# A hybrid decoder step: the ConvFFN as seven-multiplication block products in two stages, with the gated tiles kept in DRAM

## The chip, the cores and the metric

The kernel runs on one core of a Trainium2 chip. The metric is the device time of one execution in microseconds (us), median of three runs. TensorE (PE) multiplies, VectorE (DVE), ScalarE (ACT) and GpSimd (POOL) work elementwise, and SyncE (SP) issues the DMAs. SBUF is the on-chip memory; TensorE writes to PSUM, which has eight banks.

## What is computed

A prompt of 1024 tokens and eight samples of eight tokens (1088 columns together, held as features x tokens) go through two layers. Layer 0 has an attention and recurrence mixer, layer 1 a token-mixing MLP; each is followed by a gated ConvFFN with D_MODEL = 1024 and D_FF = 3072. causal_dwconv takes three taps over time and a bias; m_p and m_s are the mixer's outputs, DEPTH is 2:

```python
def conv_ffn(xn, buf, w_g, w_u, w_c, b_c, w_d):
    g = xn @ w_g
    gc, new_buf = causal_dwconv(g, buf, w_c, b_c)
    return (jax.nn.gelu(gc) * (xn @ w_u)) @ w_d, new_buf
...
    for l in range(DEPTH):
        ...
        yp = yp + m_p
        ys = ys + m_s
        fw = (w_gate[l], w_up[l], w_ffn_conv[l], b_ffn_conv[l], w_down[l])
        f_p, fb_p = conv_ffn(rmsnorm(yp, g_ffn[l]), fbuf_p, *fw)
        f_s, fb_s = conv_ffn(rmsnorm(ys, g_ffn[l]), state_ffn_conv[l], *fw)
        yp = yp + f_p
        ys = ys + f_s
```

Everything is fp32. A product is made to nearly fp32 precision with three passes over operands rounded to the fp32r type: each operand is split in a high part (its rounding, made on ACT) and a remainder (value minus high part), and the product is hi\*hi + lo\*hi + hi\*lo.

## The kernel before, in words

**Layout.** A tile is 128 features x tokens. The residual stream x lies in SBUF as eight such tiles (`core.x`, shown as x_residual, padded to 1092 columns). A weight slab is 128 x 1024. The slab loads run on SP, the high parts of slabs on ACT (L97, L104), their remainders on POOL (L108, L113).

**Gate and up.** `Ffn` works in twelve turns of two hidden tiles each. A turn has four dense products (`gu` in `Ffn.tensor`, by `dense`, L148): gate and up for two tiles, each 8 slabs deep x 3 passes x 3 column chunks (364, 364, 360) = 72 matmuls. DVE takes the gate sum from PSUM times the RMS scale in one instruction (`gate`, L2193), runs the convolution with 3 instructions over all columns and six small ones (`conv`, L2203 to L2220), ACT takes the GELU (L2112), POOL multiplies by the RMS scale that belongs to the up half (`gate_scale`, L1923), and DVE multiplies with the up sum from PSUM (L2227).

**Down.** The two hidden tiles of a turn, 256 deep, go at once into the down product, as a seven-multiplication (Strassen-Winograd) block product on 2 x 2 blocks: `tiles` makes the four block sums of the hidden tiles and seven remainders on DVE, `block` makes the four sums and the remainders of the weight blocks on POOL (L1940 to L1952). `quarter` (L1999 to L2011) runs 21 matmuls of 512 columns and four of 256 for the sample columns, four times in a turn; DVE adds each product from PSUM to x_residual (L2243). The twelfth turn's down product is dense (L2025). The quarters of turn t-1 stand between the dense products of turn t.

**Order.** Each engine has one hand-written queue; semaphores join them. On DVE a turn reads: gate, seven adds, convolution, gate, seven adds, convolution, up, seven adds, up, seven adds, tiles.

## Time and profile before

| | |
|---|---|
| median of 3 runs | 2642.78 us (2642.22 to 2642.88) |
| the profiled execution | span 2640.3 us |
| PE busy | 2589.7 us, 98% |
| DVE busy | 1606.4 us, 61% |
| POOL busy | 1133.4 us, 43% |
| ACT busy | 867.6 us, 33% |
| first ConvFFN, 638 to 1466 us | 828 us, of which PE busy 828 us |
| second ConvFFN | begins near 1792 us and runs almost to the end |

Matmuls are pipelined, so a busy PE says only that it never waited; the pace of a kind of matmul is the distance from start to start in the timeline. A mean duration on DVE or POOL contains what the instruction waited for once it had begun.

### The profile page before, as it was taken

The numbers are of one execution on the slowest core, as the hardware profiler recorded it, in microseconds if no ns is written. First come the engines' busy times: TensorE is split into PE (matmuls) and PEld (weight loads), VectorE is DVE, ScalarE is ACT, GpSimd is POOL, SyncE is SP. The second block draws the span as 40 slices with busy tenths as digits, with TensorE's granted clock in tenths as the row PEclk, the third lists the DMA queues.
The fourth block names the chain that finished last, engine by engine and source line by source line (L and its number), as shares of the span: only waits on it lengthen the run. The fifth ranks groups of instructions, "written<-read, shape, count | busy, mean of one in ns | idle before, by whom it ended". The sixth has DMA issues, their size and how long they took to land.

```text
span 2640.3 us, 42777 instructions
## 1 busy us (share of the span) xinstructions
PE 2589.7 (98%) x16013; PEld 2419.6 (92%) x16013; DVE 1606.4 (61%) x2183; ACT 867.6 (33%) x1229; POOL 1133.4 (43%) x919
## 2 busy tenths in 40 slices
PE   8999998899999999999999999999999999999999
PEld 7878886699999999999999999999999999999998
DVE  6456566533666666666676544524666677766674
ACT  5575666532222222222222524423222222222221
POOL 3233333224544454444555411344555555544541
PEclk9999999999999999999999999999999999999999
DMA  5101107731111111111111211211111111111112
GB/s 178 55 28 44 43 25 261 270 114 46 59 41 48 48 48 48 48 42 46 48 48 33 62 36 39 62 40 59 54 41 47 48 48 48 48 42 45 48 32 72
DMA packets 208445, 164.11 MB, mean 62 GB/s; under 512 B 9901, under 2 KB 182038, under 8 KB 208334
## 3 DMA queue, kind: packets, MB, share of 16 engines
q1 hardware_dynamic: 207278, 160.35, 19.5%
q10 hardware_dynamic: 576, 2.10, 0.2%
q8 instruction: 79, 1.29, 0.2%
q14 instruction: 32, 0.26, 0.0%
q0 software_dynamic: 480, 0.11, 0.0%
HBM read 147.83 MB, written 14.69 MB: 62 GB/s over the span
## 4 chain that ended last, share of the span: by engine, by line
PE 78%; DVE 0%; ACT 0%; issue 0%; DVEq 0%
PE psum_all L148 50%; PE psum_all L2011 16%; PE psum_all L2485 6%; PE psum_all L2025 2%; PE psum_all L1999 1%; PE psum_all L2001 1%; PE psum_all L2537 0%; PE psum_all L2501 0%; PE psum_all L2525 0%; PE psum_all L2355 0%; PE psum_all L2571 0%; PE psum_all L1679 0%; DVE mixed_odd L2696 0%; ACT operand_hi_a L1784 0%; PE psum_all L2542 0%
## 5 line engine op out<-in xcount | busy, mean ns | idle before, releaser
L108 POOL TENSOR_TENSOR w_lo_part<-w_raw,w_hi_part 128x1024 fp32r<-128x1024 f32 x94 | 227.4, 2419 | 578.1 <-ACT w_hi_part L104 578.1
L2243 DVE TENSOR_TENSOR x_residual<-x_residual,psum_all 128x512 f32<-128x512 f32 (+1 forms) x616 | 449.7, 760 | 19.6
L148 PE MATMUL psum_all<-operand_hi_c,w_hi_part 128*128 128x364 f32 (+1 forms) x1344 | 297.5, 330 | 0.6 <-DVE operand_lo_c L1788 0.6
L148 PE MATMUL psum_all<-operand_hi_a,w_hi_part 128*128 128x364 f32 (+1 forms) x1344 | 297.7, 330 | 0.2 <-DVE operand_lo_a L1788 0.2
L148 PE MATMUL psum_all<-operand_hi_c,w_lo_part 128*128 128x364 f32 (+1 forms) x1344 | 295.5, 328 | 0.0
L148 PE MATMUL psum_all<-operand_lo_a,w_hi_part 128*128 128x364 f32 (+1 forms) x1344 | 295.3, 328 | 0.0
L148 PE MATMUL psum_all<-operand_hi_a,w_lo_part 128*128 128x364 f32 (+1 forms) x1344 | 295.2, 328 | 0.0
L148 PE MATMUL psum_all<-operand_lo_c,w_hi_part 128*128 128x364 f32 (+1 forms) x1344 | 294.9, 327 | 0.0
L113 POOL TENSOR_TENSOR w_lo_part<-w_raw,w_hi_part 128x1024 fp32r<-128x1024 f32 x54 | 130.6, 2419 | 372.3 <-ACT w_hi_part L97 372.2
L2227 DVE TENSOR_TENSOR gate_conv_ffn<-psum_all,gate_conv_ffn 128x1092 f32<-128x1092 f32 x48 | 62.2, 1295 | 347.7 <-PE psum_all L148 347.7
L2011 PE MATMUL psum_all<-hidden_hi_ffn,w_down_hi_ffn 128*128 128x512 f32 x616 | 240.7, 391 | 0.0
L2011 PE MATMUL psum_all<-hidden_hi_ffn,w_down_lo_ffn 128*128 128x512 f32 x616 | 240.5, 390 | 0.0
L2011 PE MATMUL psum_all<-hidden_lo_ffn,w_down_hi_ffn 128*128 128x512 f32 x616 | 239.7, 389 | 0.0
L148 PEld LDWEIGHTS psum_all<-operand_hi_a,w_hi_part 128*128 128x128 f32 x1344 | 233.4, 188 | 4.2 <-DVE operand_lo_a L1788 0.5
L148 PEld LDWEIGHTS psum_all<-operand_hi_c,w_hi_part 128*128 128x128 f32 x1344 | 233.1, 188 | 4.4 <-issue 0.8
L148 PEld LDWEIGHTS psum_all<-operand_hi_c,w_lo_part 128*128 128x128 f32 x1344 | 233.4, 188 | 0.0
L148 PEld LDWEIGHTS psum_all<-operand_hi_a,w_lo_part 128*128 128x128 f32 x1344 | 233.2, 188 | 0.0
L148 PEld LDWEIGHTS psum_all<-operand_lo_a,w_hi_part 128*128 128x128 f32 x1344 | 232.2, 188 | 0.0
L148 PEld LDWEIGHTS psum_all<-operand_lo_c,w_hi_part 128*128 128x128 f32 x1344 | 232.2, 188 | 0.0
L104 ACT ACTIVATE w_hi_part<-w_raw 128x1024 fp32r<-128x1024 f32 x94 | 99.7, 1062 | 402.1 <-PE psum_all L148 402.1
L1923 POOL TENSOR_TENSOR gate_conv_ffn<-gate_conv_ffn,rms_scale 128x1092 f32<-128x1092 f32 x48 | 122.3, 2548 | 187.2 <-ACT gate_conv_ffn L2112 187.2
L1361 POOL TENSOR_TENSOR take_then_weights<-take_then_weights,x_residual 128x511 f32<-128x511 f32 (+3 forms) x96 | 96.0, 1010 | 158.4 <-DVE x_residual L1393 119.5
(354 smaller groups left out, 5031.6 us busy)
## 6 DMA issues: line engine op xcount, KB each, us to landing
w_raw<-in_w_gate_dram SPq DMA_DIRECT2D x48, 512.0 KB, 3.8
w_raw<-in_w_up_dram SPq DMA_DIRECT2D x48, 512.0 KB, 3.8
w_down_raw_ffn<-in_w_down_dram SPq DMA_DIRECT2D x44, 512.0 KB, 4.0
pages<-in_cache_k_dram SPq DMA_DIRECT2D x64, 256.0 KB, 3.5
pages<-in_cache_v_dram SPq DMA_DIRECT2D x64, 256.0 KB, 5.4
w_raw<-in_w_in_even_dram SPq DMA_DIRECT2D x20, 512.0 KB, 4.0
w_raw<-in_w_in_odd_dram SPq DMA_DIRECT2D x16, 512.0 KB, 4.8
x_spill<-x_residual SPq DMA_DIRECT2D x8, 546.0 KB, 5.3
```

The lines of the kernel that those rows point to most:

```text
L104: act.activation(dst, self.raw[:, raw, :], ACT.Copy).then_inc(self.s_hi, 1)
L108: pool.tensor_tensor(lo, self.raw[:, raw, :], hi.bitcast(F32), ALU.subtract).then_inc(self.s_lo, 1)
L113: pool.tensor_tensor(dst if dst is not None else self.lo[:, par, :], self.raw[:, par, :], (hi if hi is not None else self.hi[:, par, :]).b ...
L148: mm = pe.matmul(bank[:, c, 0:width(c)], w, x[:, chunk(c)], start=(k == 0 and step == 0), stop=(k == last and step == 2))
L1361: pool.tensor_tensor(t[:, 0:n - 1], t[:, 0:n - 1], k[:, 1:n], ALU.mult).then_inc(weighted, 1)
L1923: pool.tensor_tensor(gc, gc, self.core.rb[:, :], ALU.mult).then_inc(self.gr_ready, 1)
L1999: pe.matmul(rows, b.h_smp[:, k, :], self.blocks(b.d_hi, p, 0)[:, cols], start=start and p % 2 == 0 and k == 0, stop=False, skip_group_chec ...
L2011: mm = pe.matmul(core.ps[:, base + bank, :], wt, xt[:, x, :], start=first and step == 0, stop=step == 2, skip_group_check=True)
L2025: mm = pe.matmul(bank[:, c, 0:width(c)], wt, x[:, chunk(c)], start=(k == 0 and step == 0), stop=(k == 1 and step == 2))
L2227: dve.tensor_tensor(gc, bank[:, :, 0:CH], gc, ALU.mult).then_inc(self.evac, 1)
L2243: dve.tensor_tensor(dst, dst, src, op).then_inc(self.pair_read, 1)
L2485: mm = pe.matmul(self.core.ps[:, self.lane_bank(f), 0:width(c)], wm[:, is_u, col], xm[:, k, chunk(c)], start=k == 0 and s == 0, stop=k == ...
```

## The change

`Ffn` is replaced. A layer's ConvFFN now has two stages.

**Stage 1**, 24 jobs in 12 pairs (gate, then up, for two hidden tiles). A job multiplies a 1024 x 256 slab by all 1088 columns as a seven-multiplication product on 2 x 2 blocks: the weights in blocks of 128 columns, x in blocks of odd or even tiles by 544 columns. Its seven products have 4 x 3 x 2 = 24 matmuls of 272 columns. Weight side, per job: four block sums and seven remainders of 512 columns on POOL (`block_sums`, `block_lo`), seven high parts on ACT (`block_hi`). x side: seven operands made once in a layer, while the output projection before it ends (`tile_lo`, `open_dve`, `opening_dve`). The results go from PSUM to SBUF: four parts copied by ACT (`copy_out`), three added by DVE (`add_out`). The RMS scale of the gate is now an instruction of its own on DVE (`conv_part`, L2413), and the hidden tile is the product of two SBUF tiles (`hidden_tile`). Four block sums of the hidden tiles are made on DVE (`hidden_sum`), and the seven block operands are stored in DRAM (`store_hidden`). The space for all this is that of x: x is spilled to DRAM at the start of the layer's ConvFFN and loaded again before stage 2.

**Stage 2**, 16 jobs in 4 rounds of 4. A round takes three hidden pairs (768 deep), loads their seven operands from DRAM, splits them (high parts on ACT, remainders on DVE, `piece_hi`, `piece_lo`), and a job multiplies them by 256 columns of w_down: seven products of 3 x 3 x 2 = 18 matmuls of 272 columns, added to x by DVE (`add_residual`). Weight sums and remainders are 384 columns on POOL.

PE's waits between the seven products of a stage 1 job n stand in `tensor`: product 1 waits until the three DVE adds of job n-1 are done (`dve_out` 3n), product 3 for DVE's add of product 1. A layer has 6048 matmuls of 272 columns in place of 3456 of 364 or 360, 924 of 512, 176 of 256 and 144 dense ones. The dense projections of the mixers stay; their other passes end at column 1088 and no longer at 1092.

```diff
+    def block_sums(self, pool, n, first, second):
+        if first:
+            pool.wait_ge(self.w_in[n % 2], 16 * (n // 2 + 1))
+            if n:
+                pool.wait_ge(self.w_lo, 7 * n)
+            pool.tensor_tensor(self.sums(n, "S1"), self.part(n, 0, 1), self.part(n, 1, 1), ALU.add
+                               ).then_inc(self.w_sum, 1)
...
+    def block_lo(self, pool, n, i):
+        pool.wait_ge(self.w_hi, self.done(n, i))
...
+    def gate_scale(self, pool, t, r):
+        pool.wait_ge(self.gelu_ready, 2 * t + r + 1)
+        pool.tensor_tensor(self.conv[:, r, :], self.conv[:, r, :], self.core.rb[:, 0:USED], ALU.mult
+                           ).then_inc(self.gr_ready, 1)
...
+        for n in range(JOBS):
+            t = n // 2
+            up, last = n < JOBS1 and n % 2, n == JOBS - 1
+            for i in range(7):
+                if not last:
+                    if i < 3:
+                        self.block_sums(pool, n + 1, i == 0, (None, "S2", "S4")[i])
+                    self.block_lo(pool, n + 1, i)
+                if up and i in (3, 5):
+                    self.gate_scale(pool, t, (i - 3) // 2)
...
+        dve.wait_ge(self.dve_out, 6 * t + 2 + r)
+        g = gb[:, 2:2 + USED]
+        o.did(dve.tensor_tensor(g, g, self.core.rb[:, 0:USED], ALU.mult))
+        o.did(dve.tensor_copy(xs[:, :, 0:2], self.params.state[:, f, :].rearrange("p (s j) -> p s j", j=2)))
+        o.after()
+        if t:
+            dve.wait_ge(self.hc, 16 * t)
+        o.did(dve.tensor_scalar(gc, g, tap(2), tap(3), ALU.mult, ALU.add))
...
+        for t in range(PAIRS):
+            last = t == PAIRS - 1
+            if t:
+                for i in (1, 4, 6):
+                    self.add_out(dve, 2 * t, i)
+            self.conv_part(dve, o, t, 0)
+            self.add_out(dve, 2 * t + 1, 1)
+            self.conv_rest(dve, o, t, 0)
+            self.conv_part(dve, o, t, 1)
+            self.conv_rest(dve, o, t, 1)
+            self.add_out(dve, 2 * t + 1, 4)
+            if last:
+                self.piece_lo(dve, 0, B21)
+                self.piece_lo(dve, 0, B11)
+            self.hidden_tile(dve, t, 0)
+            self.hidden_sum(dve, t, T1)
+            self.add_out(dve, 2 * t + 1, 6)
+            if not last:
+                self.hidden_tile(dve, t, 1)
+                for i in (T3, T2, NT4):
+                    self.hidden_sum(dve, t, i)
...
+                if n < JOBS1:
+                    if i == 0:
+                        pe.wait_ge(self.act_out, 4 * n)
+                    elif i == 1:
+                        pe.wait_ge(self.dve_out, dve)
+                    elif i == 3:
+                        pe.wait_ge(self.dve_out, dve + 1)
```

On DVE, before, a gate tile's work at the start of a turn (gate_padded_ffn is the gate tile, gate_conv_ffn the convolved one):

```order
L2193 TENSOR_TENSOR gate_padded_ffn<-psum_all,rms_scale 128x1092
L2203 TENSOR_SCALAR gate_conv_ffn<-gate_padded_ffn,ffn_params 128x1092
L2204 COPY gate_sample_ffn<-ffn_state_columns 128x8x2
L2206 COPY gate_sample_ffn<-gate_padded_ffn 128x8x8
L2210 SCALAR_TENSOR_TENSOR gate_conv_ffn<-gate_padded_ffn,ffn_params,gate_conv_ffn 128x1092 x2
L2213 TENSOR_SCALAR gate_conv_ffn<-gate_sample_ffn,ffn_params 128x64
L2214 COPY new_state_columns_ffn<-gate_padded_ffn 128x2
L2215 COPY new_state_columns_ffn<-gate_sample_ffn 128x16
```

On DVE now, the end of an up job and the beginning of the next pair (gate, up and convolved tiles all lie in x_residual's space):

```order
L2401 TENSOR_TENSOR x_residual<-x_residual,psum_all 128x544
L2445 TENSOR_TENSOR x_residual<-x_residual 128x1088
L2454 TENSOR_TENSOR x_residual<-x_residual 128x544
L2401 TENSOR_TENSOR x_residual<-x_residual,psum_all 128x1088
L2445 TENSOR_TENSOR x_residual<-x_residual 128x1088
L2454 TENSOR_TENSOR x_residual<-x_residual 128x544 x3
L2401 TENSOR_TENSOR x_residual<-x_residual,psum_all 128x544 x2
L2401 TENSOR_TENSOR x_residual<-x_residual,psum_all 128x1088
L2413 TENSOR_TENSOR x_residual<-x_residual,rms_scale 128x1088
L2414 COPY gate_sample<-ffn_state_columns 128x8x2
L2418 TENSOR_SCALAR x_residual<-x_residual,ffn_params 128x1088
```

The scale by rms_scale has lost its PSUM input; both its inputs are in SBUF now. The fourth row is the last add of the up job; it stands behind the first hidden tile (second row) and its sum.

On POOL, before, the end of the first turn's weight work:

```order
L1923 TENSOR_TENSOR gate_conv_ffn<-gate_conv_ffn,rms_scale 128x1092
L108 TENSOR_TENSOR w_lo_part<-w_raw,w_hi_part 128x1024
L1923 TENSOR_TENSOR gate_conv_ffn<-gate_conv_ffn,rms_scale 128x1092
L108 TENSOR_TENSOR w_lo_part<-w_raw,w_hi_part 128x1024
L1940 TENSOR_TENSOR square_scratch<-w_down_raw_ffn 128x128
L1941 TENSOR_TENSOR square_scratch<-w_down_raw_ffn 128x128
```

On POOL now, what stands beside one up job (the weights of the gate job after it, and the two scalings of the gated tiles):

```order
L2058 TENSOR_TENSOR block_sums_a<-w_raw 128x512
L2060 TENSOR_TENSOR block_sums_a<-w_raw 128x512
L2075 TENSOR_TENSOR blocks<-w_raw,blocks 128x512
L2064 TENSOR_TENSOR block_sums_b<-block_sums_a,w_raw 128x512
L2075 TENSOR_TENSOR blocks<-w_raw,blocks 128x512
L2068 TENSOR_TENSOR block_sums_b<-w_raw,block_sums_b 128x512
L2075 TENSOR_TENSOR blocks<-block_sums_a,blocks 128x512
L2075 TENSOR_TENSOR blocks<-block_sums_b,blocks 128x512
L2081 TENSOR_TENSOR x_residual<-x_residual,rms_scale 128x1088
L2075 TENSOR_TENSOR blocks<-block_sums_b,blocks 128x512
L2075 TENSOR_TENSOR block_a_7980<-w_raw,block_a_7980 128x512
L2081 TENSOR_TENSOR x_residual<-x_residual,rms_scale 128x1088
```

A scaling stands in POOL's queue ahead of remainders that do not depend on it.

## Rows read from the trace of the kernel before

**Rows 1.** The page, part 1: busy time, share of the span and instructions of each engine.
```profile
PE 2589.7 (98%) x16013; PEld 2419.6 (92%) x16013; DVE 1606.4 (61%) x2183; ACT 867.6 (33%) x1229; POOL 1133.4 (43%) x919
```
**Rows 2.** Busy time by stretch, the first ConvFFN: PE, PEld, DVE, ACT, POOL, clock, DMA.
```profile
638.00:1466.00 828.00, 828.00 (x4692) 789.87 (x4691) 554.02 (x744) 198.67 (x273) 413.46 (x343) 1.00 0.15 47
```
**Rows 3.** PE's own waits behind 560 us (total, times, longest): the longest one.
```profile
PE psum_all L2355 <- DVE y_rows L2381: 1.6, 2, 0.9
```
**Rows 4.** Timeline of PE (start, duration, then what): matmuls of 364, 256 and 512.
```profile
801.19 0.66 PE L148 MATMUL psum_all<-operand_hi_a,w_lo_part 128*128 128x364 f32 x3
...
803.67 0.28 PE L1999 MATMUL psum_all<-w_down_hi_ffn,hidden_sample_ffn 128*128 128x256 f32 x1
...
804.14 0.40 PE L2011 MATMUL psum_all<-hidden_hi_ffn,w_down_hi_ffn 128*128 128x512 f32 x1
...
805.97 0.39 PE L2011 MATMUL psum_all<-hidden_lo_ffn,w_down_hi_ffn 128*128 128x512 f32 x1
```
**Rows 5.** Timeline of DVE and of POOL around 862 us.
```profile
861.99 1.36 DVE L2203 TENSOR_SCALAR gate_conv_ffn<-gate_padded_ffn,ffn_params 128x1092 f32<-128x1092 f32 x1
863.27 1.26 DVE L2204 COPY gate_sample_ffn<-ffn_state_columns 128x16 f32 x1
...
861.47 1.29 POOL L1949 TENSOR_TENSOR w_down_lo_ffn<-w_down_raw_ffn,w_down_hi_ffn 128x512 fp32r<-128x512 f32 x1
862.72 1.77 POOL L1952 TENSOR_TENSOR w_down_lo_ffn<-square_scratch,w_down_hi_ffn 128x512 fp32r<-128x512 f32 x1
```
**Rows 6.** Timeline of DVE and of POOL around 1437 us.
```profile
1437.16 1.66 DVE L2284 TENSOR_TENSOR hidden_lo_ffn<-gate_conv_ffn,hidden_hi_ffn 128x1092 fp32r<-128x1092 f32 x1 [1.74 <-ACT hidden_hi_ffn L2137]
...
1435.26 5.84 POOL L108 TENSOR_TENSOR w_down_lo_ffn<-w_raw,w_down_hi_ffn 128x1024 fp32r<-128x1024 f32 x2 [8.43 <-ACT w_down_hi_ffn L104]
```
**Rows 7.** Timeline of DVE and of POOL around 995 us.
```profile
994.43 5.35 DVE L2243 TENSOR_TENSOR x_residual<-x_residual,psum_all 128x512 f32<-128x512 f32 x7
...
994.86 2.41 POOL L108 TENSOR_TENSOR w_lo_part<-w_raw,w_hi_part 128x1024 fp32r<-128x1024 f32 x1
997.22 0.47 POOL L1940 TENSOR_TENSOR square_scratch<-w_down_raw_ffn 128x128 f32<-128x128 f32 x1
997.64 0.47 POOL L1941 TENSOR_TENSOR square_scratch<-w_down_raw_ffn 128x128 f32<-128x128 f32 x1
```
**Rows 8.** Groups by shape on DVE behind 560 us (count, busy, mean ns, idle before).
```profile
L2243 DVE TENSOR_TENSOR x_residual<-x_residual,psum_all 128x512 f32<-128x512 f32 x528 | 342.4, 683 | 12.6
L2210 DVE SCALAR_TENSOR_TENSOR gate_conv_ffn<-gate_padded_ffn,ffn_params,gate_conv_ffn 128x1092 f32<-128x1092 f32 x96 | 130.5, 1359 | 12.3 <-DVE gate_sample_ffn L2206 6.1
L2243 DVE TENSOR_TENSOR x_residual<-x_residual,psum_all 128x1024 f32<-128x1024 f32 x88 | 107.5, 1221 | 6.9
L2213 DVE TENSOR_SCALAR gate_conv_ffn<-gate_sample_ffn,ffn_params 128x64 f32<-128x64 f32 x48 | 15.6, 324 | 1.8
```
**Rows 9.** One line's instructions on DVE or POOL: duration ns min/median/max.
```profile
L2218 DVE SCALAR_TENSOR_TENSOR gate_conv_ffn<-gate_sample_ffn,ffn_params,gate_conv_ffn x24: 283/286/1270, 661.9 to 1422.5; 128x64 f32<-128x64 f32 x24
...
L1923 POOL TENSOR_TENSOR gate_conv_ffn<-gate_conv_ffn,rms_scale x24: 2532/2552/2576, 663.7 to 1424.3; 128x1092 f32<-128x1092 f32 x24
...
L1949 POOL TENSOR_TENSOR w_down_lo_ffn<-w_down_raw_ffn,w_down_hi_ffn x44: 1282/1292/1322, 682.0 to 1412.4; 128x512 fp32r<-128x512 f32 x44
```
**Rows 10.** Groups by shape on ACT behind 560 us, as rows 8.
```profile
L2119 ACT ACTIVATE w_down_hi_ffn<-w_down_raw_ffn 128x512 fp32r<-128x512 f32 x88 | 54.9, 624 | 176.1 <-PE psum_all L2011 176.1
L2112 ACT ACTIVATE gate_conv_ffn<-gate_conv_ffn 128x1092 f32<-128x1092 f32 x48 | 53.6, 1117 | 232.9 <-DVE gate_conv_ffn L2220 232.9
```
**Rows 11.** Timeline of PE, and stretches as rows 2: an idle TensorE and its clock.
```profile
472.70 2.22 PE L1017 MATMUL psum_all<-identity,pages 128*128 128x128 f32 x12 [1.52 <-DVE x_residual L1526]
...
474.00:476.00 2.00, 2.00 (x12) 2.00 (x11) 0.78 (x2) 0.78 (x2) 0.00 (x0) 0.50 0.83 203
477.00:480.00 3.00, 3.00 (x28) 0.98 (x20) 0.00 (x0) 0.39 (x2) 0.00 (x0) 1.00 0.77 259
466.00:468.00 2.00, 1.61 (x12) 0.85 (x8) 1.97 (x2) 1.44 (x4) 0.00 (x0) 1.00 1.06 405
```

More of the change, by code:

```diff
@@ L1792, in scalar @@
         w, n0 = self.core.w, self.n0
-        for m in range(KT):
-            w.split_hi(act, n0 + m + 2, (n0 + m + 2) // 2, m % 2, (w.used, n0 + m + 3 - self.skew))
-            self.lead.tile_act(act, m)
+        for m in range(KT - 2):
+            w.split_hi(act, n0 + m + 2, (n0 + m + 2) // 2, m % 2, self.job_done(m))
+            self.ffn.tile_act(act, m)
             if m == 0:
@@ new lines, in multiply @@
+    def multiply(self, pe, n, i, ready=None):
+        name, first = self.GROUPS[i]
+        b = self.banks[name]
+        depth = self.depth(n)
+        x_hi, x_lo = self.operand(n, i, 0), self.operand(n, i, 1)
+        w_hi, w_lo = self.block(n, i, 0), self.block(n, i, 1)
+        order = [(q, s) for s in range(3) for q in range(depth)]
+        if ready:
+            order = [(q, s) for q in range(depth) for s in range(3)]
+        mm = None
+        for at, (q, s) in enumerate(order):
+            if ready and s == 0:
+                ready(q)
+            wt, xt = ((w_hi, x_hi), (w_lo, x_hi), (w_hi, x_lo))[s]
+            for h in range(2):
+                mm = pe.matmul(self.core.ps[:, b + h, 0:HB], wt[:, q * P:(q + 1) * P], xt[:, q, HB * h:HB * (h + 1)],
+                               start=first and at == 0, stop=at == len(order) - 1, skip_group_check=True)
+        mm.then_inc(self.product, 1)
@@ new lines, in tile_dve, with tile_lo @@
+    def tile_dve(self, dve, m, held=None):
+        for which, (i, h) in enumerate(((B21, 0), (B22, 1)) if m % 2 else ((B11, 0),)):
+            if not (m == held and which):
+                self.tile_lo(dve, m, which, i, h)
+    def tile_lo(self, dve, m, which, i, h):
+        q = m // 2
+        dve.wait_ge(self.b_hi, 3 * q + 1 + (m % 2) + which)
+        dve.scalar_tensor_tensor(self.operand(0, i, 1)[:, q], self.half(self.core.x[:, m, :], h), self.gain(m),
+                                 self.operand(0, i, 0)[:, q].bitcast(F32), ALU.mult, ALU.subtract).then_inc(self.b_lo, 1)
@@ new lines, in add_out @@
+    def add_out(self, dve, n, i):
+        dve.wait_ge(self.product, self.done(n, i))
+        dve.wait_ge(self.act_out, 4 * n + {1: 1, 4: 3, 6: 4}[i])
+        if i == 6:
+            dst = self.target(n, 1).rearrange("p (c h n) -> p c h n", c=2, h=2)
+            src = self.group("a").unsqueeze(1).to_broadcast((P, 2, 2, HB))
+        else:
+            dst = self.half(self.target(n, 0), i == 4).rearrange("p (h n) -> p h n", h=2)
+            src = self.group("a" if i == 1 else "bb")
+        dve.tensor_tensor(dst, dst, src, ALU.add).then_inc(self.dve_out, 1)
@@ new lines, in add_residual @@
+    def add_residual(self, dve, n, i):
+        m = n - JOBS1
+        base, p = 3 * JOBS1 + 7 * m, m % QUARTERS
+        top, low = self.core.x[:, 2 * p, :], self.core.x[:, 2 * p + 1, :]
+        if m < QUARTERS and i == 0:
+            dve.wait_ge(self.x_back[p], 32)
+        dve.wait_ge(self.product, self.done(n, i))
+        if i in (1, 4, 6):
+            dve.wait_ge(self.dve_out, base + {1: 1, 4: 4, 6: 6}[i])
+        if i == 6:
+            dst = low[:, 0:USED].rearrange("p (c h n) -> p c h n", c=2, h=2)
+            src = self.group("a").unsqueeze(1).to_broadcast((P, 2, 2, HB))
+        else:
+            tile, h = ((top, 0), (top, 0), (low, 1), (top, 1), (top, 1), (low, 0))[i]
+            dst = self.half(tile, h).rearrange("p (h n) -> p h n", h=2)
+            src = self.group(self.GROUPS[i][0])
+        dve.tensor_tensor(dst, dst, src, ALU.add).then_inc(self.dve_out, 1)
@@ L2827, in _ @@
             params1.load(sp)
-            out1.slabs(sp)
+            out1.sync(sp)
             ffn1.sync(sp)
```

1325 lines of the change are left out of this document (718 added, 607 removed).

## The prediction

> **What bounds the kernel now.** Read the busy shares first: PE is busy for 98% of the span, DVE for 61%, POOL for 43% [rows 1]. Then the stretch of the first ConvFFN: 828 us, and PE busy in all of them [rows 2]. Then PE's own waits: behind 560 us the longest kind comes to 1.6 us in total [rows 3]. So the ConvFFNs are bound by PE's stream, and since a busy PE is no pace, the pace comes from distances of starts [rows 4]: 15 matmuls of 364 or 360 columns in 803.67 - 801.19 = 2.48 us, 165 ns each; 4 of 256 in 0.47 us, 118 ns; 8 of 512 in 1.83 us, 229 ns. From 364 to 512 that is 0.43 ns a column and a fixed part of some 10 to 15 ns.
>
> **PE's new stream.** No row has 272 columns. From the 256 row, 118 + 16 x 0.43 = 125 ns; down from the 364 row, 165 - 91 x 0.42 = 127 ns. I take 127 (it is the longer, and the 256 row is only four matmuls); 125 to 129 is the range. A stage 1 product has 24 matmuls, 3.05 us; a job 7 of them, 21.35 us; a pair 42.7 us. A stage 2 job is 126 x 0.127 = 16.0 us. A layer: 6048 x 0.127 = 768 us against 828 [rows 2], 60 us less, 120 us for both. The seven-for-eight saving on gate and up is partly paid back by the narrower matmul.
> The Trainium skill (TensorE: Matmul & The Clock Gate, section "Wait — 56ns, not 53.3ns?") puts the fixed part of a warm matmul at about 2.5 ns. By that a 272-column one would be an estimated 116 ns and a layer 700 us. The rows above show 10 to 15 ns for these fp32r matmuls with a weight load each, so the page's figure isn't used.
>
> **What DVE and POOL do to each other.** This decides the case. At 861.99 a DVE tensor_scalar over 1092 columns begins while POOL's remainder (861.47 + 1.29) runs; POOL's next one, begun at 862.72, takes 1.77 us in place of a median of 1.29 [rows 5, 9]. The 16-column copy behind it takes 1.26 us and ends with that POOL instruction. At 1437.16 a DVE tensor_tensor with both inputs in SBUF takes 1.66 us, and two POOL remainders together 5.84 us where one alone takes 2.41 [rows 6, 7]: 1.02 us too long. A small DVE instruction of 0.28 us takes up to 1.27 [rows 9]. But seven DVE adds with one input in PSUM take 5.35 us beside a POOL instruction that still takes 2.41 [rows 7]. I read: POOL's tensor_tensors exclude DVE instructions with two SBUF inputs, and copies and plain tensor_scalars in SBUF; whoever came first finishes, then the other. PSUM adds are free of it.
> The change moves work under this lock. Pure durations: POOL 1.26 us start to start for 512 columns [rows 5], hold 1.15; 2.55 us for a gate scaling [rows 9], hold 2.4. A pair has 22 of the first (8 sums, 14 remainders; that a sum of four pieces of 128 costs no more than a remainder is assumed) and 2 of the second: 30 us held. DVE: 683 and 1221 ns for 512 and 1024 columns [rows 8] are 1.05 ns a column and 0.15 fixed, so 544 columns take 0.7 us and 1088 1.3, held for 0.6 and 1.15; a tap with a second tensor is alike (1359 ns for 1092, [rows 8]); the first tap, a tensor_scalar, runs at double pace, since at 862.72 it had still to run and was done at 863.35: 0.6 us [rows 5]. Per tile: RMS scale 1.15, three taps 0.6 + 1.15 + 1.15, small ones 0.2; per pair two tiles, two hidden tiles 2.3 and four sums 2.3: 13 us held. Together 43 us of the 42.7 that PE gives; before, a turn of two hidden tiles had 828 / 12 = 69 us.
>
> **One pair walked through.** Zero is the end of the gate job's last product. ACT takes 0.63 us for a high part and for a 544-column copy, 1.1 for a GELU [rows 10]. In DVE's queue stand: last add of the gate job, first tile's scale and two taps, add of the up job's product 1, rest of the first convolution, the whole second one, add 4, hidden tile, hidden sum, last add.
> - Last add 0 to 1.3. POOL's remainder of the last block 0.7 to 1.9. Scale 1.9 to 3.1, POOL sum to 4.2, copy, POOL sum to 5.4, first tap to 6.0, POOL remainder to 7.1, copy, POOL sum to 8.3, second tap to 9.5, add to 10.2. Product 3 could begin at 9.15 and waits 1.1 us.
> - POOL remainder to 10.5, third tap to 11.75, POOL sum to 12.8, two copies and POOL's remainder to 14.1, small ones to 14.8. GELU to 15.9; POOL's remainder meanwhile to 15.8, the second tile's scale to 17.0, gate scaling (POOL) to 19.3, copy, remainder to 20.5, first tap to 21.1, remainder to 22.3; then POOL waits for the second GELU, and DVE alone finishes at 26.5.
> - Add 4 to 27.2, hidden tile to 28.4, POOL's second gate scaling to 30.8, hidden sum to 31.4, last add to 32.7. PE ended the up job at 10.25 + 4 x 3.05 = 22.45 and product 0 of the next at 25.5; its product 1 needs that last add: 7.2 us of waiting.
> - Hidden tile and three sums, each behind one POOL instruction, to 40.0; the add of product 1 to 40.7, and product 3, ready at 38.85, waits 1.9 us. Four products more: the pair ends at 52.95.
> So a pair takes 53.0 us, 10.2 of them waits of PE, 245 us in 24 pairs. Without the lock the same DVE queue takes about 18 us and all three waits vanish. ACT has some 15 us of work in a pair and SP's stores stay behind loads needed a job later; 47 MB more a layer are some 50 GB/s in 900 us, where the trace has 405 [rows 11]: no term.
> PE's idle time has a second price: behind 1.52 us of waiting in a thin stretch its granted clock is 0.50, that is 1.2 of 2.4 GHz, from 474 to 476, and 1.00 from 477 [rows 11]. Here some 3 us at half clock behind the 7 us wait cost 1.7 us in products 1 and 2, which the 1.9 us wait absorbs: I take nothing; if it doesn't, 0 to 2 us a pair.
>
> **The rest of a layer.** Opening: T2's remainder needs x tile 7, seven DVE instructions and 2176 columns after it, some 13 us, where PE has three products, 9.1 us; with T3's end 7 us (0 to 15). Step to stage 2: add 4, two remainders of 1632 columns (683 x 1632 / 512 is 2.2 us at most, 1.8 by the slope), hidden tile and sum stand ahead of the last add, and each product waits for its own remainder; some 22 us of waits, 9 of which are already in the twelfth pair: 13 us (5 to 25). Three changes of round: seven remainders, 12.6 us, and 5.2 us of adds plus turns with POOL in a 16 us job: 4 us each, 12 (0 to 25). Work on the next mixer's operands in the last round: 3 us. Other stage 2 jobs wait for nothing: their adds read PSUM.
>
> **The sum.** 12 x 53.0 = 636; 16 x 16.0 = 256; 7 + 13 + 12 + 3 = 35: 927 us a layer against 828, 99 more, 198 for both. The profiled execution's span, 2640.3 us, becomes 2838; the median lies 2.5 above that span: 2841, given as **2840**. Its own range, with pairs of 50 to 56 us and the bounds above: 2760 to 2920.
>
> **The rivals.**
> *The lock doesn't reach PE* (faster): POOL has slack inside a job, its blocks are needed a job later, and if DVE mostly goes first, its chain from the gate job's end to the last add stays under 24.4 us (21.35 + 3.05), the point from which PE waits. Then pairs take 42.7 to 43.5: 768 to 780 plus 25 = 800 a layer, 2585; 2550 if the steps cost little. For it: DVE's own work there is 18 us. Against it: the copy at 863.27 lost its turn to a POOL instruction that already waited [rows 5], and POOL waits nearly always here.
> *Half of it*: the chain takes 28 us in place of 33 (fewer encounters, or POOL idle for longer than I have). Pairs of 47.5: 570 + 256 + 35 = 861, two layers 66 more: 2710.
> *It is worse*: the clock falls at each wait and isn't absorbed, and four-piece sums cost 1.7 us as the four single ones before did (a 128-column one starts 0.42 us after another, [rows 7]); pairs of 57: 684 + 256 + 60 = 1000, 2985.
>
> **How the numbers follow.** Forecast 0.60, no effect of the lock 0.17, half 0.15, worse 0.08. Range for 8 in 10: 2600 to 2910, which leaves out the first rival's most and the worst case. A measurement of this kernel can tell about 0.2% from no change, 5 us. Faster: the first rival and a fifth of the half case, 0.20; the same 0.02; slower 0.78.
>
> **What would show it.** In the profile after: PE's waits led by a DVE add on x_residual, some 7 us and 24 times, and one of 1 to 2 us twice a pair; pairs 53 us apart; DVE copies of 16 columns and taps with means far over their minima; POOL over 70% busy; PE's clock under 1.00 in many stretches. A start-to-start of 272-column matmuls of 125 to 129 ns shows the first step; 116 would refute it. If DVE's waits on POOL don't show in those means, the forecast is wrong from its base; if they do and PE still waits under 2 us a pair, the walk is.

## The result and the profile after

The changed kernel takes 2859.69 us (median of four runs, 2859.14 to 2864.93) against 2642.59 for the kernel before on the same chip: 1.0829 times as long, 95% interval 1.0814 to 1.0844. The forecast was 2840 and its range 2600 to 2910. The profiled execution has a span of 2857.4 us.

The page's part 1, and the row of TensorE's clock in its 40 slices, answer to [rows 1]:
```profile
PE 2534.9 (89%) x18693; PEld 2421.1 (85%) x18693; DVE 1870.5 (65%) x1846; ACT 1081.0 (38%) x1611; POOL 1764.4 (62%) x1175
...
PEclk9999999998899899899999999998998998999999
```
PE issues more matmuls than before and is busy 55 us less, so the span, 217 us longer, lies in PE's idle time. PE's own waits over the whole run (total, times, longest), which answer to [rows 3]:
```profile
PE psum_all L2136 <- DVE x_residual L2401: 206.2, 55, 11.1
PE psum_all L2136 <- DVE x_residual L1827: 14.5, 2, 7.2
PE psum_all L2136 <- DVE ffn_x L2370: 14.4, 2, 7.5
PE psum_all L2136 <- DVE down_x_ffn L2086: 9.1, 2, 4.8
```
L2401 is the add from PSUM in `add_out`. One pair in PE's timeline (start, duration, then what; in brackets the idle time ahead and what ended it), as [rows 4] are read:
```profile
884.38 8.03 PE L2136 MATMUL psum_all<-ffn_x,blocks 128*128 128x272 f32 x48 [7.27 <-DVE x_residual L2401]
892.76 6.24 PE L2136 MATMUL psum_all<-ffn_x,blocks 128*128 128x272 f32 x48 [0.35 <-DVE x_residual L2401]
898.84 3.16 PE L2136 MATMUL psum_all<-ffn_x,block_a 128*128 128x272 f32 x24
901.84 3.16 PE L2136 MATMUL psum_all<-ffn_x,block_s 128*128 128x272 f32 x24
904.84 9.16 PE L2136 MATMUL psum_all<-ffn_x,blocks 128*128 128x272 f32 x72
915.54 6.24 PE L2136 MATMUL psum_all<-ffn_x,blocks 128*128 128x272 f32 x48 [1.53 <-DVE x_residual L2401]
921.62 3.16 PE L2136 MATMUL psum_all<-ffn_x,block_a 128*128 128x272 f32 x24
924.62 3.16 PE L2136 MATMUL psum_all<-ffn_x,block_s 128*128 128x272 f32 x24
927.62 3.16 PE L2136 MATMUL psum_all<-ffn_x,blocks 128*128 128x272 f32 x24
938.14 12.13 PE L2136 MATMUL psum_all<-ffn_x,blocks 128*128 128x272 f32 x76 [7.36 <-DVE x_residual L2401]
```
The pair is 938.14 - 884.38 = 53.76 us. Its three waits are ahead of product 1 of the gate job (7.27), product 3 of the gate job (0.35) and product 3 of the up job (1.53). Between 898.84 and 904.84 two products of 24 matmuls start 3.00 us apart, 125 ns a matmul.

DVE in the same pair, same columns, from the gate job's last add on:
```profile
905.04 1.29 DVE L2401 TENSOR_TENSOR x_residual<-x_residual,psum_all 128x1088 f32<-128x1088 f32 x1 [5.28 <-PE psum_all L2136]
...
914.68 0.71 DVE L2401 TENSOR_TENSOR x_residual<-x_residual,psum_all 128x544 f32<-128x544 f32 x1
...
922.41 2.51 DVE L2414 COPY gate_sample<-ffn_state_columns 128x16 f32<-128x16 f32 x1
...
936.71 1.27 DVE L2401 TENSOR_TENSOR x_residual<-x_residual,psum_all 128x1088 f32<-128x1088 f32 x1
```
The last add of the up job ends at 937.98; PE was ready for it at 930.8. A copy of 16 columns takes 2.51 us on the way. What it waited for, on DVE and on POOL:
```profile
920.11 2.38 DVE L2413 TENSOR_TENSOR x_residual<-x_residual,rms_scale 128x1088 f32<-128x1088 f32 x1
...
921.41 3.47 POOL L2081 TENSOR_TENSOR x_residual<-x_residual,rms_scale 128x1088 f32<-128x1088 f32 x1
```
This is one exchange of turns: DVE's scale runs until 922.49; POOL's scaling, begun at 921.41, ends at 924.88, 2.4 us after DVE's; and the copy behind DVE's scale, begun at 922.41, ends at 924.92, with POOL's instruction. Groups on DVE by shape from 700 to 1150 us (count, busy us, mean ns, idle before), as [rows 8]:
```profile
L2454 DVE TENSOR_TENSOR x_residual<-x_residual 128x544 f32<-128x544 f32 x33 | 67.0, 2029 | 1.1
L2413 DVE TENSOR_TENSOR x_residual<-x_residual,rms_scale 128x1088 f32<-128x1088 f32 x17 | 36.6, 2155 | 0.0
L2421 DVE SCALAR_TENSOR_TENSOR x_residual<-x_residual,ffn_params 128x1088 f32<-128x1088 f32 x17 | 32.5, 1914 | 0.6
...
L2414 DVE COPY gate_sample<-ffn_state_columns 128x16 f32<-128x16 f32 x17 | 29.1, 1713 | 0.0
...
L2419 DVE COPY gate_sample<-x_residual 128x64 f32<-128x64 f32 x17 | 24.2, 1426 | 0.0
L2401 DVE TENSOR_TENSOR x_residual<-x_residual,psum_all 128x544 f32<-128x544 f32 x33 | 23.5, 712 | 52.0 <-PE psum_all L2136 52.0
```
The hidden sum of 544 columns with both inputs in SBUF means 2029 ns, the add of 544 columns with one in PSUM 712.

Last, PE's clock behind the long wait, in stretches as [rows 11]:
```profile
884.40:888.40 4.00, 4.00 (x18) 4.00 (x19) 3.96 (x2) 0.00 (x0) 4.00 (x3) 0.51 0.21 84
888.40:892.40 4.00, 4.00 (x32) 3.79 (x31) 3.93 (x4) 0.64 (x1) 4.00 (x3) 1.00 0.14 56
```
After 7.27 us of idle time the granted clock is 0.51, 1.2 of 2.4 GHz, and 18 matmuls start in 4 us in place of 32.

### The profile page after: what moved, and what is told of

It is laid out like the page before. It is cut to its first block, busy times and chain, and to the rows that moved or that the text cites. A ratio compares the mean times of both kernels' runs of the same rounds, so it can differ in the third digit from the quotient of the medians.

```text
span 2857.4 us, 46273 instructions
## 1 busy us (share of the span) xinstructions
PE 2534.9 (89%) x18693; PEld 2421.1 (85%) x18693; DVE 1870.5 (65%) x1846; ACT 1081.0 (38%) x1611; POOL 1764.4 (62%) x1175
## 4 chain that ended last, share of the span: by engine, by line
PE 46%; DVE 23%; issue 8%; POOL 3%; ACT 1%; DVEq 0%; ACTq 0%; POOLq 0%
PE psum_all L2136 32%; PE psum_all L2697 6%; PE psum_all L148 6%; DVE x_residual L2401 3%; DVE x_residual L2431 3%; DVE x_residual L2413 2%; DVE x_residual L2418 2%; DVE gate_sample L2414 2%; DVE x_residual L2445 2%; DVE gate_sample L2419 2%; DVE x_residual L2421 1%; DVE x_residual L2454 1%; DVE x_residual L2434 1%; DVE new_state_columns L2435 1%; POOL blocks_down L2075 1%
## 5 line engine op out<-in xcount | busy, mean ns | idle before, releaser
L2136 PE MATMUL psum_all<-ffn_x,blocks 128*128 128x272 f32 x5760 | 802.3, 302 | 240.0 <-DVE x_residual L2401 203.0
L2136 PEld LDWEIGHTS psum_all<-ffn_x,blocks 128*128 128x128 f32 x5760 | 784.6, 202 | 253.3 <-POOL block_s L2075 169.8
L2136 PE MATMUL psum_all<-down_x_ffn,blocks_down 128*128 128x272 f32 x2880 | 380.2, 292 | 31.0 <-DVE down_x_ffn L2086 9.1
L2136 PEld LDWEIGHTS psum_all<-down_x_ffn,blocks_down 128*128 128x128 f32 x2880 | 371.0, 191 | 37.3 <-issue 28.7
L113 POOL TENSOR_TENSOR w_lo_part<-w_raw,w_hi_part 128x1024 fp32r<-128x1024 f32 x52 | 126.9, 2441 | 358.4 <-ACT w_hi_part L97 358.3
L2473 DVE TENSOR_TENSOR x_residual<-x_residual,psum_all 128x544 f32<-128x544 f32 (+1 forms) x224 | 178.6, 798 | 223.1 <-PE psum_all L2136 222.0
L2401 DVE TENSOR_TENSOR x_residual<-x_residual,psum_all 128x544 f32<-128x544 f32 x144 | 129.9, 902 | 281.8 <-PE psum_all L2136 265.2
L2081 POOL TENSOR_TENSOR x_residual<-x_residual,rms_scale 128x1088 f32<-128x1088 f32 x48 | 154.0, 3208 | 113.2 <-ACT x_residual L2261 112.1
L2454 DVE TENSOR_TENSOR x_residual<-x_residual 128x544 f32<-128x544 f32 x96 | 185.1, 1928 | 3.2
L2697 PE MATMUL psum_all<-operand_a,w_hi_part 128*128 128x364 f32 (+1 forms) x672 | 169.9, 331 | 0.0
L909 PE MATMUL psum_all<-in_hi_even,w_hi_part 128*128 128x384 f32 (+1 forms) x456 | 157.0, 344 | 1.2 <-DVE xb_padded L1430 0.6
```

Source lines behind the costliest of these rows:

```text
L113: pool.tensor_tensor(dst if dst is not None else self.lo[:, par, :], self.raw[:, par, :], (hi if hi is not None else self.hi[:, par, :]).b ...
L909: mm = pe.matmul(bank(key, 0, b - a), wt[:, n % 2, col], xt[:, k, a:b], start=k == 0 and s == 0, stop=k == KT - 1 and s == 2)
L2081: pool.tensor_tensor(self.conv[:, r, :], self.conv[:, r, :], self.core.rb[:, 0:USED], ALU.mult).then_inc(self.gr_ready, 1)
L2136: mm = pe.matmul(self.core.ps[:, b + h, 0:HB], wt[:, q * P:(q + 1) * P], xt[:, q, HB * h:HB * (h + 1)], start=first and at == 0, stop=at = ...
L2401: dve.tensor_tensor(dst, dst, src, ALU.add).then_inc(self.dve_out, 1)
L2454: dve.tensor_tensor(dst, x, y, op).then_inc(self.hid, 1)
```

## The experiments

Theory: DVE and POOL take turns at SBUF, so that each DVE instruction with two SBUF inputs, and each copy, waits for a POOL instruction; this makes the chain to the up job's last add longer than the 24 us that PE leaves it. Rivals: the add comes too late by its place in DVE's queue, whatever the lengths; or DVE's own work is too long. The edits are shown shortened, and "..." stands for lines left out.

**One cause taken away: the remainders don't read SBUF.**
```
-  pool.tensor_tensor(block(n, i, 1), source(n, i), block(n, i, 0), ALU.subtract)
+  for q in range(4):                       # stage 1 only
+      mm = pool.memset(block(n, i, 1)[:, q * P:(q + 1) * P], 0.0)
```


> The changed kernel with one edit: in stage 1 POOL's fourteen weight remainders a pair are four memsets of 128 columns each in place of one subtraction of 512, so the remainders of gate's and up's weights are zero (that part of the computation is left out); POOL still writes as many columns, but reads nothing from SBUF there. Theory (POOL's SBUF reads exclude DVE's two-input instructions and copies): POOL holds the lock for 8 sums and 2 scalings a pair, 14 us in place of 30; the 16-column copies on DVE fall from a mean of 1.66 us to under 0.9, the last add comes some 6 us earlier, PE's 7.3 us wait falls to 0 to 3, pairs take 43 to 47 us in place of 53.8, and the whole some 2600 to 2700 us. Rival (DVE's queue is too long by itself, in the order it is written): nothing changes, 2860. Rival (POOL's own lateness holds PE): PE's waits on DVE stay and those on POOL go, under 10 us in all.

Measured: 2703.34 us, 1.023 of before (1.021 to 1.0251). 156 us of the loss are gone, and the time lies just above the expected range. The pair is 47.7 us: the 7.3 us wait has become 1.73, and 1.99 and 1.24 us are left ahead of the two products 3. The profile puts the 1.99 down to POOL (in all such waits of the run 39.9 us, 20 times), but the POOL instruction that ended then, at 880.05, fills a block of the next job; DVE's add of the up job's product 1, which product 3 waits for, ended at 880.02, and PE went on at 880.16. So it is the changed kernel's 1.53 us wait ahead of that product, and the third outcome expected as possible, lateness of POOL itself, isn't shown. The sums and the gate scaling still read SBUF, and DVE's hidden sums still mean 2026 ns, while its 16-column copy fell from 1713 to 718.

**All of POOL's reads in stage 1 taken away.**
```
+  def fill(pool, dst, inc):                # block sums, remainders, gate scaling
+      four memsets of a quarter of dst's columns each
```


> The changed kernel with everything that GpSimd reads from SBUF in stage 1 taken away: the remainders, the block sums S1 to S4 and the gate scaling are each written as four memsets of a quarter of the columns. Left out of the computation are therefore stage 1's remainders, its block sums and the scaling of the gate; every wait, every weight-block conversion, all 48 DVE instructions of a pair and all TensorE work stand. Theory (DVE and GpSimd exclude each other instruction by instruction when both read SBUF, and that alone makes DVE late): DVE's instructions all fall to their own lengths (16 columns far under 1 us, sums L2459-like and taps to some 1.3 us), TensorE hardly waits inside a pair, a pair takes 42.7 to 44.5 us instead of 53.8 and 47.7 without the remainders alone; 24 pairs x (53.8 - 43.5) = 247, and some 12 from the two openings: 2600, range 2575 to 2640. Rival (what is left of the wait is the chain product, copy, add, three taps, product and comes from the order of DVE's work): the pair stays near 47.7 and the time near 2700.

Measured: 2564.37 us, 0.9707 of before (0.9686 to 0.9727), below the expected range. PE's row from 700 to 1150 us (PE, PEld, DVE, ACT, POOL, clock, DMA share, GB/s), and under it three groups of DVE as above:
```profile
700.00:1150.00 450.00, 450.00 (x3579) 450.00 (x3578) 243.01 (x352) 157.56 (x254) 183.63 (x995) 1.00 0.29 101
```
```profile
L2478 DVE TENSOR_TENSOR x_residual<-x_residual 128x544 f32<-128x544 f32 x40 | 29.0, 724 | 1.4
L2437 DVE TENSOR_TENSOR x_residual<-x_residual,rms_scale 128x1088 f32<-128x1088 f32 x21 | 27.0, 1285 | 0.0
...
L2438 DVE COPY gate_sample<-ffn_state_columns 128x16 f32<-128x16 f32 x21 | 5.2, 249 | 0.0
```
PE never stops; the pair is 42.3 us. DVE does 352 instructions in 243 us where the changed kernel did 290 in 349 (its row from 700 to 1150 is shown below). Its program is the same, and so is its order, so the order alone does no harm and DVE's own work fits. POOL still writes SBUF, by 988 memsets that hold it for 176 of the 450 us, and the two-input instructions never lengthen beside them: the 40 sums lie between 724 and 726 ns, the 21 scales between 1283 and 1286. It is POOL's reading that excludes these. The short copies do still wait for a memset: the 2-column copy takes 0.33 us beside one (at 730.14) and 0.16 beside none (at 723.82).

The edit changes one thing more: POOL's busy time falls from 346 to 184 us, so its results are ready earlier. But in the changed kernel DVE stood idle ahead of the hidden tiles, the ones that need POOL's result, for only 1.8 us of the 450, so this can't be the gain.

**The order of DVE's adds.** In the changed kernel add 4 and add 6 of the up job stand behind the whole second gate tile.
```
   self.conv_part(dve, o, t, 1)
+  self.add_out(dve, 2 * t + 1, 4)
+  self.add_out(dve, 2 * t + 1, 6)
   self.conv_rest(dve, o, t, 1)
-  self.add_out(dve, 2 * t + 1, 4)
   ...
   self.hidden_tile(dve, t, 0)
   self.hidden_sum(dve, t, T1)
-  self.add_out(dve, 2 * t + 1, 6)
```


> The changed kernel with DVE's adds 4 and 6 of the up job moved ahead, between the second tile's first two taps and the rest of its convolution. Nothing is left out. Theory (PE's 7.3 us wait is for the position of the last add in DVE's queue, behind instructions that the lock draws out): that wait falls to under 1.5 us. But the hidden tile and sums come later by as much, and the gate job's product 3 waits for the add behind them: from 0.4 us to 3 to 6. Pairs 49 to 51 us in place of 53.8, some 2740 to 2800 us. Rival (the wait just moves): 2860. Rival (the add's position is all there is): pairs of 44, 2640.

Measured: 2881.42 us, 1.0904 (1.0873 to 1.0934): 0.8% slower than the changed kernel. This expectation failed, and the rival that the wait just moves was right, but for the 22 us more. The wait went to the next add in the queue:
```profile
892.52 7.71 PE L2136 MATMUL psum_all<-ffn_x,blocks 128*128 128x272 f32 x48 [8.57 <-DVE x_residual L2401]
...
947.12 3.29 PE L2136 MATMUL psum_all<-ffn_x,blocks 128*128 128x272 f32 x13 [8.56 <-DVE x_residual L2401]
```
This is product 3 of the gate job, which waits for add 1 of the same job, now behind everything that was put off. So that add goes forward too:
```
   the edit above, and
-  for i in (1, 4, 6): self.add_out(dve, 2 * t, i)
+  for i in (4, 6): self.add_out(dve, 2 * t, i)
   ...
   self.hidden_sum(dve, t, T1)
+  self.add_out(dve, 2 * t + 2, 1)
   self.hidden_tile(dve, t, 1)
```


> As the run before, and the gate job's add of product 1 stands ahead of the second hidden tile and the last three sums. Nothing is left out. Theory: both waits go, what is left is product 3 of the up job, 1.5 us, and what a later POOL adds to the next pair, 0 to 3 us: pairs 44 to 47 us, 2625 to 2700 us. Rival (DVE and POOL together are saturated, the pair is bound by the lock's total of 43 us plus turns lost, whatever the order): pairs of 50 and more, over 2770.

Measured: 2729.42 us, 1.0329 (1.0312 to 1.0347), somewhat above the expected range. The pair is 47.7 us, with 2.4 and 1.3 to 1.5 us of waits. The 96 matmuls behind the 2.36 us wait take 917.93 - 904.44 = 13.49 us in place of 12.0, since the clock falls there too (904.40 to 906.40, as above):
```profile
904.40:906.40 2.00, 1.96 (x9) 1.99 (x10) 1.90 (x5) 0.00 (x0) 0.00 (x0) 0.50 0.65 221
```

**Copies that don't take turns.** The four small DVE copies of a gate tile, written as a sum over an axis of one element.
```
-  dve.tensor_copy(dst, src)
+  dve.tensor_reduce(dst, src.unsqueeze(-1), AxisListType.X, ALU.add)
```


> The changed kernel with the four small copies of each hidden tile on DVE (16, 64, 2 and 16 columns) written as tensor_reduce over an axis of one element, which gives the same values. Nothing is left out. Theory (a copy in SBUF waits for POOL's turn, a tensor_reduce doesn't): the three copies of means 1.66, 1.38 and 0.74 us fall to 0.2 to 0.3 each; part of it comes back as a longer wait of the next instruction, since POOL still takes turns; PE's 7.3 us wait falls to 1 to 5 us, pairs 48 to 52 us, 2720 to 2820 us. Rival (the reduce waits as the copy does): the means stay, 2860. Rival (all waits come back in the taps): means fall and the time stays.

Measured: 2823.7 us, 1.0686 (1.0664 to 1.0707), 36 us less than the changed kernel and just above the expected 2720 to 2820. Groups on DVE, 700 to 1150 us:
```profile
L2426 DVE SCALAR_TENSOR_TENSOR x_residual<-x_residual,ffn_params 128x1088 f32<-128x1088 f32 x17 | 46.4, 2732 | 0.6
...
L1639 DVE TENSOR_REDUCE gate_sample<-x_residual 128x64 f32<-128x64 f32 x17 | 3.5, 206 | 0.0
L1639 DVE TENSOR_REDUCE gate_sample<-ffn_state_columns 128x16 f32<-128x16 f32 x17 | 2.7, 157 | 0.0
```
The 16-column copy fell from 1713 ns to 157, the 64-column one from 1426 to 206. But the tap behind them, 1914 ns in the changed kernel (L2421 there), is now 2732: where a copy had waited for POOL, the next instruction that takes turns waits. The four copies of a tile became 3.4 us shorter; its other convolution instructions and the scale became 2.5 us longer together by their means. That leaves 0.9 a tile, 1.7 a pair, and the pair (52.1 us) became 1.6 shorter. The rival that the waits come back in the taps was right for the larger part.
The Trainium skill (SBUF — State Buffer, section "Who interferes with whom") says that tensor_reduce on trn2 never contends with GpSimd. The 157 and 206 ns agree.

**Edits together.** First the early adds and the copies by reduction.

> The two edits that gave something, together: the adds of product 4 and 6 of the up job and of product 1 of the next gate job earlier in DVE's queue (2729 alone), and the four small copies of a gate tile as sums over an axis of one element (2824 alone against 2860). Nothing is left out. Theory of the lock with turns: short copies that wait a GpSimd instruction each cost some 8 x 0.6 us of DVE a pair, but part of it comes back in the next two-input instructions; the wait that is left after the early adds is 3.8 us a pair, and the copies can give at most 1.5 (what they gave alone: 36 us in 24 pairs) : 2690 to 2725. Rival (the early adds left TensorE waiting on something that the copies don't stand in front of): 2725 to 2735, as without the copies.

Measured: 2662.83 us, 1.0081 (1.0064 to 1.0098), better than either theory had it. The two edits gave 130 and 36 us alone and 197 together.

The third edit moves the gate scaling to DVE, so that one multiplication by DVE takes the place of one by POOL:
```
-  if up and i in (3, 5): self.gate_scale(pool, t, (i - 3) // 2)
   def hidden_tile(self, dve, t, r):
+      self.gate_scale(dve, t, r)
```
With the early adds:

> The early adds, and the scaling of the gate tile by the token's factor on DVE just ahead of the product with u, instead of on GpSimd (L2081, two of 3.24 us in a pair). Nothing is left out. Theory (what counts is the time that both engines together hold the way to SBUF): a GpSimd multiplication of 1088 columns of some 2.4 us on its own goes, a DVE one of some 1.3 us comes, so the sum held falls by 2.2 us a pair, up to 24 x 2.2 = 53 us of the 84 us of waits that are left: 2680 to 2725. Rival (what counts is the length of DVE's own queue, 41.5 us of 54 busy): 2 x 1.3 us or more are added to it ahead of the adds, and the time rises by 24 x 1 to 2.6: 2750 to 2790.

Measured: 2669.08 us, 1.0102 (1.0085 to 1.0119), below the range of the first theory, which was the nearer by far. From 700 to 1150 us, the changed kernel's row and this one's:
```profile
700.00:1150.00 450.00, 370.58 (x2781) 366.44 (x2779) 349.33 (x290) 126.94 (x203) 345.99 (x202) 0.92 0.21 75
```
```profile
700.00:1150.00 450.00, 424.68 (x3329) 419.22 (x3328) 418.43 (x357) 147.82 (x239) 363.35 (x220) 1.00 0.26 91
```
DVE is busy for 93% of the stretch and PE waits less than in the changed kernel; with the early adds alone DVE and PE were busy for 400 and 411 us, so the moved scaling by itself raised both. A busy share that includes turns waited for says little on how full an engine is.

All three edits:

> All three edits: early adds, gate scaling on DVE, the four small copies as sums over an axis of one element. Nothing is left out. If the time held by both engines together decides, it is the shortest of the kernels that compute everything, 2650 to 2700, near the 2643 of the kernel before; if DVE's own queue decides, 2710 to 2770, above the run with the early adds and the copies alone.

Measured: 2610.86 us, 0.9887 (0.987 to 0.9903): computing everything, this kernel is faster than the kernel before, by 1.1%, and it is below the expected range too. Its pair:
```profile
885.96 6.24 PE L2139 MATMUL psum_all<-ffn_x,blocks 128*128 128x272 f32 x48 [0.33 <-DVE x_residual L2404]
...
928.52 6.24 PE L2139 MATMUL psum_all<-ffn_x,blocks 128*128 128x272 f32 x48 [0.32 <-DVE x_residual L2404]
```
42.56 us, one wait of 0.3.

The two small edits without the early adds:

> Gate scaling on DVE and the four copies as sums over an axis of one element, with DVE's order as the change has it (no early adds). Nothing is left out. If the order is a condition of its own (the add of product 6 of the up job stands behind the whole second gate tile, so it comes after product 3 of the next gate job could start however short each instruction is), a wait of 2 us or more stays in each pair: 2660 to 2730. If only the time held by both engines counts (and the early adds merely sheltered the critical ones from it), it is as with all three edits: 2605 to 2630.

Measured: 2793.47 us, 1.0579 (1.0561 to 1.0596). The order is a condition of its own once the turns are there, and more so than expected: without the early adds the pair keeps one wait of 6.3 us, and its price is higher than its length:
```profile
869.61 14.86 PE L2139 MATMUL psum_all<-ffn_x,blocks 128*128 128x272 f32 x96 [6.30 <-DVE x_residual L2404]
884.30 3.16 PE L2139 MATMUL psum_all<-ffn_x,block_a 128*128 128x272 f32 x24
...
920.80 14.87 PE L2139 MATMUL psum_all<-ffn_x,blocks 128*128 128x272 f32 x96 [6.34 <-DVE x_residual L2404]
```
Start to start the 96 matmuls behind it take 884.30 - 869.61 = 14.69 us, where at 125 ns each they would take 12.0: 2.7 us go to the lower clock. The pair, 920.80 - 869.61 = 51.2 us, is within 0.1 of 42.3 + 6.3 + 2.7.

The gate scaling alone:

> Gate scaling on DVE alone; copies and order as the change has them. Nothing is left out. With the early adds this edit gave 60 us (2729 to 2669). If the gain is from the time held by both engines, it gives at least as much where the wait is longer, since nothing absorbs it: 2860 less 60 to 110 is 2750 to 2800. If DVE's own queue counts, the added multiplication of at least 1.3 us stands ahead of the adds that TensorE waits for, and nothing or a loss comes: 2860 to 2900.

Measured: 2826.08 us, 1.0693 (1.0675 to 1.071), 34 us less than the changed kernel. The sign is that of the turns; the size, below the 60 to 110 us expected, shows that a saving is worth less where the order still holds the add back.

Medians of the kernels that compute everything, in us (each batch ran beside the kernel before, at 2641.2 to 2642.65):

| edit | adds as in the change | adds early |
|---|---|---|
| neither | 2859.7 | 2729.4 |
| copies by reduction | 2823.7 | 2662.8 |
| gate scaling on DVE | 2826.1 | 2669.1 |
| both | 2793.5 | 2610.9 |

The two small edits give 66 us together in the left column and 119 in the right. Why they give more beside the early adds, no run takes apart.

**The ends of stage 1.** On top of the three edits, first the opening: the last mixer tile's add from PSUM ahead of the three T2 sums.
```
   self.ffn.open_dve(dve)                   # now without its three t2_sum
   ... add of the last tile (L1827) ...
+  for q in range(3): self.ffn.t2_sum(dve, q)
```


> All three edits (2611), and at each stage 1's opening the last mixer tile's own add from PSUM ahead of the three T2 sums instead of behind them; nothing is left out. TensorE waits there 7.2 us for that add, then 6.6 for T2's remainder, 3.1 for a copy of ACT. If the opening is bound by the run of sums that DVE must have done by the fourth product (DVE is busy without a gap from 633 to 667 us in the changed kernel), the first wait shrinks by 5 us and the second grows by as much: within 2 us of 2611. If each wait is its own, 2 x 5 us are won: 2601.

Measured: 2608.45 us, 0.9872 (0.9856 to 0.9888). The interval overlaps that of the run without the edit. In the first layer's opening PE waited 7.2 us for the tile's add and 6.6 for T2's remainder; now:
```profile
PE psum_all L2142 <- DVE ffn_x L2350: 5.6, 1, 5.6
PE psum_all L2142 <- DVE ffn_x L2374: 4.2, 1, 4.2
PE psum_all L2142 <- ACT x_residual L2254: 3.1, 1, 3.1
PE psum_all L2142 <- DVE x_residual L1832: 1.9, 1, 1.9
```
The wait moved to other instructions of the same DVE stretch, 13.8 us became 11.7. As expected, the opening is bound by DVE's run of sums as a whole.

Then the remainder of stage 2's first operand ahead of the last `conv_rest`, with the opening as above:
```
+  if last: self.piece_lo(dve, 0, B21)
   self.conv_rest(dve, o, t, 1)
-  if last: self.piece_lo(dve, 0, B21)
```


> As the run with the changed opening, and the remainder of the first operand of stage 2 ahead of the rest of the second gate tile's convolution in the last pair instead of behind it; nothing is left out. TensorE waited 12.4 us over both layers for that remainder. Theory (that wait is only the place in DVE's queue, some five instructions of the convolution ahead of it): 6 to 10 us less than the run with the changed opening. Rival (ACT's conversion or the following adds are late in its place): within 2 us of it.

Measured: 2609.21 us, 0.988 (0.9863 to 0.9896), no difference. Around the first layer's step (1180 to 1225 us) one wait of 6.6 us for the remainder and 2.4 for residual adds (the run with the changed opening) became 3.2 and 5.1. The rival held: the wait was taken over by the next instructions.

## Why the prediction was right

*What bounds PE before, and PE's new stream.* Right. 272-column matmuls start 125 to 126 ns apart (3.00 to 3.02 us a product) where 127 was taken. The fixed part that the rows of before showed stays with these matmuls, though it is smaller than the prediction's text has it: by its own 0.43 ns a column 165 ns leave 9 and 125 ns leave 8, not 10 to 15. The sum doesn't use it. The estimate of 116 ns that the prediction worked out from the Trainium skill (TensorE: Matmul & The Clock Gate, section "Wait — 56ns, not 53.3ns?") isn't borne out.

*The turns of DVE and POOL.* This was the base, and it held: 16-column copies with a mean of 1713 ns, sums of 544 columns with a mean of 2029 where they take 724 without POOL's reads, PSUM adds untouched at 712. The run without POOL's reads is the proof: 2860 becomes 2564 with DVE's program as it was. One assumption was right too: the sums of four pieces cost no more than a remainder; other sums mean up to 2353 ns with their turns. From 690 to 1300 us (duration ns min/median/max):
```profile
L2064 POOL TENSOR_TENSOR block_sums_b<-block_sums_a,w_raw x12: 1012/1284/1293, 700.1 to 1288.6; 128x512 f32<-128x512 f32 x11, 128x384 f32<-128x384 f32 x1
```

*One pair walked through.* With zero at the gate job's last product (904.84 above):

| | predicted | measured |
|---|---|---|
| add of up product 1 ends | 10.2 | 10.55 |
| wait before up product 3 | 1.1 | 1.5 |
| second convolution done | 26.5 | 27.0 |
| last add ends | 32.7 | 33.1 |
| wait before gate product 1 | 7.2 | 7.3 |
| wait before gate product 3 | 1.9 | 0.35 |
| pair | 53.0 | 53.8 |

The first tap was taken too short: 0.6 us held, where it takes 0.85 undisturbed (the run without POOL's reads). The clock was taken as absorbed by the third wait, and for the most part it was: the 48 matmuls behind the long wait took 892.76 - 884.38 - 0.35 = 8.03 us and the next 48 took 898.84 - 892.76 = 6.08, so 2.0 went to the clock (1.7 in the prediction), and the third wait is 1.55 us shorter than the walk had it. With the third wait gone, as in the run with the old order and both small edits, its 2.7 us stand in the pair undiminished.

*The rest of a layer.* Here the sizes were off and partly cancelled: the opening and the first pair took 7 us more than summed, the other eleven pairs 12 more, stage 2 8 less. That the forecast lies within 0.7% of the measured time is in this part luck. Opening: 7 us were taken (0 to 15). The first layer's first pair runs from 641.21 to 708.34, 67.1 us, where the sum had 53.0 + 7 = 60:
```profile
641.21 3.23 PE L2136 MATMUL psum_all<-ffn_x,blocks 128*128 128x272 f32 x24 [0.84 <-POOL blocks L2075]
651.68 8.29 PE L2136 MATMUL psum_all<-ffn_x,blocks 128*128 128x272 f32 x48 [7.24 <-DVE x_residual L1827]
666.90 4.57 PE L2136 MATMUL psum_all<-ffn_x,blocks 128*128 128x272 f32 x24 [6.93 <-DVE ffn_x L2370]
...
685.45 17.06 PE L2136 MATMUL psum_all<-ffn_x,blocks 128*128 128x272 f32 x120 [3.14 <-ACT x_residual L2248]
```
The wait for T2's remainder is the one foreseen. The step missed the ten sums that `open_dve` puts ahead of the last mixer tile's own add; they take 17.1 us with turns, and PE stands 7.2 us. The other eleven pairs take (1303.8 - 708.3) / 11 = 54.1 us, 1.1 more than the walk; the second pair's long wait is 11.1. Stage 2 from 1303.8 on takes 276 us against 284: the step costs 4.3, 3.2 and 1.8 us of waits, and the changes of round about 2 us each in place of 4 (at the first 0.5 for an add, 0.7 for which the profile shows no cause, 0.65 for POOL). The first layer is 939 us against 927, the span 2857.4 against 2838.

*The rivals.* That the turns don't reach PE was priced at 2585; with POOL's reads gone the chip gave 2564, 1% below. The half case, 2710 with pairs of 47.5 us, is about where the runs with one strong edit lie (2703 and 2729, pairs of 47.7); these are other kernels, so this says only that the price fits such pairs. The dearer sums of the worst case didn't come.

How much of the gain of the early adds is the waits and how much the clock, the traces tell for one pair: waits of 9.2 us and 2.0 us of slower matmuls in the changed kernel, 3.7 and 1.5 with the early adds. Of the 6.1 us by which the pair shrank, 5.5 are waits and 0.5 is clock.

## What to carry to other kernels

Add up what DVE holds with two SBUF inputs and what POOL holds reading SBUF over one turn of the loop; when the sum nears TensorE's turn, walk the queue with turns and look for the add that PE needs, for it will be late though both engines look two thirds busy. Then do three things at once, since each alone gave 1 to 5% and all together 8.7%: put the adds that PE waits for ahead of the work nobody waits for, all of them and not only the one that is late now; give an elementwise operation to the engine that holds the way for the shorter time; and write small copies in a form that takes no turn. A single late instruction moved forward only hands its wait to the next (2881, 2609), so count what must be done by that time, not what stands in front.
